# The opening of a three-block network: an input unit loaded ahead of two modulation units, and the context's affine step on ScalarE

## The chip, the cores and the metric

One core of one Trainium2 chip runs the whole program. The metric is the device time of one execution in microseconds (us). Of the kernel before, three runs are given; their median is what changes are measured against. A separate profiled execution gives the trace.

## What is computed

Three network blocks follow one another on a sequence of 256 tokens of width 1024, all in float32. The change touches the opening of the first block only:

```python
sh1, sc1, gt1, ... = split(silu(c) @ w_ada + b_ada)          # modulation of the tokens ("lat")
sh1c, sc1c, ...    = split(silu(c_ctx) @ w_ada + b_ada)      # modulation of the context ("ctx")
h_ctx = rms_norm(ctx, g_mix) * (1 + sc1c) + sh1c
h_lat = rms_norm(x, g_mix) * (1 + sc1) + sh1
u_c, q_c, v_c, ... = split_proj(h_ctx @ w_in)                # w_in: 1024 x 3072
u_l, q_l, v_l, ... = split_proj(h_lat @ w_in)
```

After it come a Fourier mixer and a gated linear recurrence over context and tokens, an output projection, a mixture of 16 experts (their weights, some 550 MB, are by far the largest part of what is read), then a second block with attention, spatial gating and a feed-forward part, and a third with two layers of attention and short convolutions.

## The kernel before, in words

**Layout.** Activations lie feature-major: 1024 features are 8 chunks of 128 partitions, 256 tokens along the free axis. `X` holds the tokens, `CTX` the context. Weights come through a ring of four slots (`ring`); a unit is what one slot holds. `w_ada`'s first 2048 columns are eight units of 1 MB (one per chunk of the input features); `w_in` is nine units of up to 384 columns (1.5 MB). The plan deals slots out in the order 2, 3, 1, 0 (`CYCLE`, line 119), so the first input unit takes the slot of modulation unit 4, the second that of unit 5, the third that of unit 6, the fourth that of unit 7. SyncE issues all these loads from one program in order; before a load it waits until the unit that had the slot has been used (`load`, L532 to L535).

**Opening.** SyncE loads X, small constants, CTX and then the modulation units (`load_ada(0)`, L558). PE sums squares of X (L893), multiplies modulation units 0 to 3 (`first_unit`, L715 to L722), sums squares of CTX, multiplies units 4 to 7, and turns the result into columns (`first_turn`, L729) after ScalarE has copied the rows out (L1391). Between them VectorE squares X (L1715), scales it by the reciprocal root (L1728, L1731), squares CTX and takes its reciprocal root too, but leaves CTX itself unscaled.

**Split weights.** A product in float32 is made of three matmuls in a reduced type: high part times high part, low times high, high times low (`parts`, L771). For every 128 columns of weights (a split, 128x1024) ScalarE copies the high part into `w_hi` (`high_parts`, L1329) and VectorE subtracts it from the weights into `ring_lo` (`low_parts`, L1706). `w_hi` has four places, so the high part of split s waits for the last block that uses split s - 4. The activations are split likewise: ScalarE copies high parts (L1408), VectorE subtracts (L1740), into `x_parts` and `ctx_parts`.

**Modulation.** `mod_in(0)` (L1770 to L1785) adds the bias to the turned columns, for the context (`modc`, L1782) and the tokens (`mod`, L1783), and two small steps (L1763) make the scales. `modulate_chunk` (L1927) is the affine step of one chunk of 128x256 on VectorE, for tokens and context. Before `mod_in(0)` VectorE makes the low parts of two splits, and that of a third after two chunks of tokens.

**Input blocks.** The first projection has 32 blocks (`in1_items`) in this order: 0 to 2 (unit 0) together, chunk by chunk (`k_outer`, L776 to L792), then 3 to 5 and 6, 7 one after another (L837), all for the tokens; then turned blocks 8 to 11, where the activation is the stationary operand (L831), for tokens and context in turn, 8 being the first turned one and 9 the first that reads the context; then 12 to 31 (L837). An unturned block is 24 matmuls, a turned one 48. Block 9 waits for all eight low chunks of the context (L912). PE also makes the bias rows after block 4 (L924), `gate_sum` after block 26 and `ada_sum` after block 29 (L754).

For each block in turn ScalarE takes the high part three splits on, evacuates the block (`evacuate`, L1335 to L1342), and in the first four blocks copies the high parts of two context chunks (L1428); at block 4 it also evacuates the bias rows (L1396). VectorE runs its own loop over the blocks (L1940 to L1956): the low part three splits on, then in the first four blocks two context chunks: two normalisations (L1945), two affine steps (L1931), two low parts (L1740). Then it adds modulation shares: the rest of `w_ada` comes as 32 tiles of 128x1024 through four buffers, each multiplied by its condition and added up on VectorE (`add_to`, L1793 to L1800) at the block that `THIRD_AT` (L126) gives it, from block 3 to block 26. SyncE loads a share (L572) when the one four before it has been added. `gate_sum` needs the last share of the gate's columns, `ada_sum` the last of all.

**Order on SyncE.** After the fourth input unit come the first four shares; later units and shares alternate by `thirds_until`, which loads a share once the block of the one four places before it is not past the block given. So all shares up to a block are waited for ahead of the next unit.

**After.** The mixers' and the output projection's PE work follows; slots of later weights come free by PE's progress, and the experts' weights stream behind them.

Of the kernel before, what the change touches and what calls it, by code (L numbers as in the profile page):

```python
# [14 lines left out]
P = 128  # L15
# [48 lines left out]
def constants():  # L64
# [21 lines left out]
    for n in range(LEVELS - 1):  # L86
# [38 lines left out]
ADA_FIRST = 2048  # L125
THIRD_AT = sorted([(3 + n, n % THIRDS, n // THIRDS) for n in range(THIRDS * KD)] +  # L126
                  [(i, THIRDS, k) for k, i in enumerate((8, 9, 10, 11, 14, 17, 20, 23))])
GATE_AT = 26
SUM_AT = 29
# [3 lines left out]
TAIL = 1  # L133
CTX_STEP = 2
CTX_ITEMS = KD // CTX_STEP
PAIRS = ATT // 2
# [120 lines left out]
def build(nc, inp, scratch, out):  # L257
# [56 lines left out]
    with ctx:  # L314
# [212 lines left out]
        def _(sp):  # L527
# [17 lines left out]
            def load_dense(units, w, after=lambda i: None):  # L545
                view = w.rearrange("(k p) n -> p k n", p=P)
                for i, g in enumerate(units):
                    load(g["u"], slot(g["u"], KD, g["w"]), view[:, :, g["c0"]:g["c0"] + g["w"]])
                    after(i)
# [7 lines left out]
            sp.dma_start(OFFS[0:33, :], inp["offsets"]).then_inc(S("rel_in"), 16)  # L557
            load_ada(0)  # L558

# [23 lines left out]

            load_dense(in1, inp["w_in"][0], after_in1)
            for kc in range(RING):
# [107 lines left out]
        def _(pe):  # L693
# [205 lines left out]
            pe.wait_ge(S("conds_ready"), 1)  # L899
            for kc in range(4):  # L900
                first_unit(kc)
            sum_squares()
            for kc in range(4, KD):
                first_unit(kc)
# [390 lines left out]
        def _(act):  # L1295
# [91 lines left out]
            root()  # L1387
            root()
            name, n = plan.used[ada[0][KD - 1]]
            act.wait_ge(S(name), n)  # L1390
# [12 lines left out]

            def high_modulated(which, c):

                src, dst = ((H, X_HI), (HC, C_HI))[which]
                act.wait_ge(S("h_chunk"), KD * which + c + 1)
                mark(act.activation(dst[:, c, :], src[:, c, :], ACT.Copy), "x_high")  # L1408

            high_parts(starts["in1"] + 3)  # L1410
            for c in range(KD):
                high_modulated(0, c)
            done = 0
            for g in in1:
                for it in g["items"]:
# [11 lines left out]
                    if done < CTX_ITEMS:  # L1427
                        for c in range(CTX_STEP):  # L1428
                            high_modulated(1, CTX_STEP * done + c)
                    if done == BROW_AT:  # L1430
# [251 lines left out]
        def _(dve):  # L1682
# [87 lines left out]
            def mod_in(p):  # L1770

                waits("turned", p + 1)
                bias = [V("b_ada", 0, 24), V("b_ada", 24, 24), V("b_ada_2", 0, 24), V("b_ada_2", 24, 24),
                        V("b_ada_3", 0, 24), mod[:, 4, :], V("b_ada_3", 24, 24)][p]
                k = 24
                if p == 0:
                    k = 16
                    bias = bias[:, 0:k]
                v = ps[:, 4, 0:4 * k].rearrange("p (q j c) -> p j q c", q=k // CG, j=CG)
                bias = bias.rearrange("p (j q) -> p j q", j=CG)  # L1780
                if p == 0:
                    link(tt(modc[:, 0:k].rearrange("p (j q) -> p j q", j=CG), v[:, :, :, 1], bias, ALU.add))  # L1782
                link(tt(mod[:, (0, 1, 2, 3, 4, 4, 5)[p], 0:k].rearrange("p (j q) -> p j q", j=CG),  # L1783
                        v[:, :, :, (0, 0, 2, 2, 3, 3, 3)[p]], bias,
                        ALU.add), "mod_ready")  # L1785

            x_squares = [0]
# [132 lines left out]
            normalise(CTX, CTX, chunks=False)  # L1920
            low_parts(starts["in1"] + 2)
            mod_in(0)
            scale_columns(V("g_mix", 0, 8), mod[:, 0, 8:16])
            scale_columns(V("g_mix", 0, 8), modc[:, 8:16])
            shift_scale = ((mod[:, 0, 0:8], scl[:, 1, :]), (modc[:, 0:8], scl[:, 2, :]))

            def modulate_chunk(which, c):  # L1927

                src, dst = ((XN, H), (CTX, HC))[which]
                shift, scale = shift_scale[which]  # L1930
                link(ts(dst[:, c, :], src[:, c, :], scale[:, c:c + 1], shift[:, c:c + 1], ALU.mult, ALU.add), "h_chunk")  # L1931

            modulate_chunk(0, 0)
            modulate_chunk(0, 1)
            low_parts(starts["in1"] + 3)
            for c in range(KD):
                if c + 2 < KD:
                    modulate_chunk(0, c + 2)
                low_modulated(c, H, X_HI, X_LO)
            for i, it in enumerate(in1_items):  # L1940
                low_parts(it["s"] + HI)
                if i < CTX_ITEMS:
                    chunks = range(CTX_STEP * i, CTX_STEP * i + CTX_STEP)
                    for c in chunks:
                        link(tt(CTX[:, c, :], CTX[:, c, :], rs[:, 0:T], ALU.mult), "normed")  # L1945
                    for c in chunks:
                        modulate_chunk(1, c)
                    for c in chunks:
                        low_modulated(c, HC, C_HI, C_LO)
                for n, (at, c, k) in enumerate(THIRD_AT):  # L1950
# [551 lines left out]
```

## Time and profile before

| | us |
|---|---|
| Median of 3 runs | 2242.11 (2239.89 to 2244.26) |
| Span of the profiled execution | 2235.1 |
| Time of the profiled execution outside its span | not given |
| PE busy | 1703.4 (76% of the span) |
| VectorE (DVE) busy | 809.1 (36%) |
| ScalarE (ACT) busy | 514.1 (23%) |
| Start of the first input block | 42.40 |
| Start of the first turned block | 74.73 |
| First expert's wait for weights in the chain | 324.56 |

The span is what the trace covers; the runs' times also hold what lies around it. Busy time is an average over very different stretches, so the trace is read by stretch. In the rows, PE is the matmul engine, PEld its weight loads, SPq what SyncE issues to the DMA queue, ACTq the same for ScalarE. L12 is line 12 of the kernel; a helper's line stands for all its uses. An arrow names what ended the idle time before an instruction. PEclk is the granted clock of TensorE: 1.00 is 2.4 GHz, 0.50 is 1.2 GHz. Instructions on one engine overlap at their ends, so the distance from start to start (the pitch) is what a step costs, rather than its duration.

### The profile page before, as it was taken

The page shows a single profiled execution, that of the slowest core. Times are in us where ns is not written, and L with a number is a line of the kernel's source. Part 1 is how long each engine was busy: PE and PEld are TensorE (multiplying, and loading weights), DVE is VectorE, ACT ScalarE, POOL GpSimd, SP SyncE. Part 2 cuts the span into 40 slices and gives each one's busy share as a digit, 9 for nine tenths or more (in the row PEclk, how much of TensorE's full clock was granted, in tenths as well). Part 3 has the DMA queues.
Part 4 walks back from the last instruction along what each step waited for, and adds up shares of the span by engine and source line. Part 5 has one row for each costly group of instructions (what it writes and reads, how often), then busy time and mean ns, then how long its engine had stood idle before and what let it go on. Part 6 is the DMA issues. An engine that isn't in the chain of part 4 may idle for free.

```text
span 2235.1 us, 33839 instructions
## 1 busy us (share of the span) xinstructions
PE 1703.4 (76%) x14882; PEld 1178.4 (53%) x14882; DVE 809.1 (36%) x1271; ACT 514.1 (23%) x833; POOL 60.7 (3%) x94
## 2 busy tenths in 40 slices
PE   5999987656656665665665666565999999999897
PEld 4896843222222321331332232222898999998897
DVE  5766730100100100010010010010875789688777
ACT  2420210000000000000000000000673664365664
POOL 0015000000000000000000000000000000000000
PEclk8999987778777777777877777787999999999998
DMA  9777989999999999999999999999645659754541
GB/s 363 294 262 298 373 354 430 434 430 433 432 431 432 431 432 435 428 432 435 430 432 433 432 432 432 431 432 402 207 148 202 198 164 368 251 169 127 167 133 66
DMA packets 138725, 760.69 MB, mean 340 GB/s; under 512 B 7911, under 2 KB 96743, under 8 KB 106888
## 3 DMA queue, kind: packets, MB, share of 16 engines
q1 hardware_dynamic: 134968, 754.13, 83.6%
q10 hardware_dynamic: 3664, 5.24, 0.7%
q8 instruction: 68, 1.11, 0.2%
q14 instruction: 25, 0.20, 0.0%
HBM read 756.20 MB, written 3.14 MB: 340 GB/s over the span
## 4 chain that ended last, share of the span: by engine, by line
DMA 48%; PE 45%; DVE 5%; ACT 1%; issue 1%; SPq 0%; DVEq 0%; ACTq 0%
DMA ring<-in_w_exp_down 26%; PE ps L837 19%; DMA ring<-in_w_exp_up 18%; PE ps L1280 4%; PE ps L1144 4%; PE ps L1137 4%; PE ps L788 3%; DMA w_hi_raw<-in_w_exp_up 3%; PE ps L710 1%; PE ps L1261 1%; PE ps L983 1%; DVE ring_lo L1706 1%; PE ps L831 1%; PE ps L1189 1%; PE ps L1200 0%
## 5 line engine op out<-in xcount | busy, mean ns | idle before, releaser
L1144 PE MATMUL ps<-arena,const 128*32 128x352 f32 x2816 | 332.1, 631 | 250.4 <-DMA arena<-in_w_exp_up 132.8
L1144 PEld LDWEIGHTS ps<-arena,const 128*32 128x32 f32 x2816 | 105.3, 140 | 466.2 <-DMA arena<-in_w_exp_up 166.1
L1706 DVE TENSOR_TENSOR ring_lo<-ring,w_hi 128x1024 fp32r<-128x1024 f32 x220 | 267.3, 1218 | 49.0 <-ACT w_hi L1329 47.9
L837 PE MATMUL ps<-u_hi,w_hi 128*128 128x258 f32 x960 | 277.2, 289 | 1.2 <-DVE ring_lo L1706 1.1
L837 PE MATMUL ps<-u_lo,w_hi 128*128 128x258 f32 x960 | 272.9, 284 | 0.0
L2111 DVE TENSOR_TENSOR tail<-tail,ps 128x704 f32<-128x704 f32 x15 | 13.3, 887 | 715.4 <-PE ps L1144 715.4
L837 PE MATMUL ps<-u_hi,ring_lo 128*128 128x258 f32 x960 | 269.2, 280 | 0.0
L1329 ACT ACTIVATE w_hi<-ring 128x1024 fp32r<-128x1024 f32 x220 | 230.1, 1050 | 72.9 <-PE ps L1280 34.6
L1144 PE MATMUL ps<-ring,const 128*32 128x352 f32 x1024 | 125.5, 654 | 80.4 <-DMA ring<-in_w_exp_up 40.2
L837 PEld LDWEIGHTS ps<-u_hi,w_hi 128*128 128x128 f32 x960 | 181.6, 189 | 7.3 <-issue 5.2
L837 PEld LDWEIGHTS ps<-u_hi,ring_lo 128*128 128x128 f32 x960 | 183.3, 191 | 0.0
L837 PEld LDWEIGHTS ps<-u_lo,w_hi 128*128 128x128 f32 x960 | 180.4, 188 | 0.0
L1137 PE MATMUL ps<-ring,const 128*32 128x256 f32 x1536 | 131.9, 513 | 57.3 <-DMA ring<-in_w_exp_down 57.2
L1137 PE MATMUL ps<-arena,const 128*32 128x256 f32 x896 | 86.5, 551 | 63.4 <-DMA arena<-in_w_exp_down 63.4
L1144 PEld LDWEIGHTS ps<-ring,const 128*32 128x32 f32 x1024 | 39.3, 144 | 167.3 <-issue 58.6
L1492 ACT ACTIVATE const<-ps 128x256 f32<-128x256 f32 x16 | 6.1, 383 | 517.3 <-PE ps L1093 517.3
L1137 PEld LDWEIGHTS ps<-ring,const 128*32 128x32 f32 x1536 | 60.5, 143 | 113.5 <-DMA ring<-in_w_exp_down 61.0
L1487 ACT ACT_TABLE_LOAD x15 | 19.2, 1283 | 405.6 <-PE ps L1144 405.6
L837 PE MATMUL ps<-x_parts,w_hi 128*128 128x256 f32 x592 | 109.2, 283 | 3.1 <-DVE ring_lo L1706 3.1
L2115 DVE TENSOR_TENSOR const<-ps,tail 128x256 f32<-128x256 f32 x15 | 6.4, 424 | 279.9 <-PE ps L1102 279.9
L1137 PEld LDWEIGHTS ps<-arena,const 128*32 128x32 f32 x896 | 42.6, 156 | 106.8 <-issue 71.4
L837 PEld LDWEIGHTS ps<-x_parts,w_hi 128*128 128x128 f32 x592 | 92.3, 188 | 6.0 <-DVE ring_lo L1706 5.5
(311 smaller groups left out, 2417.0 us busy)
## 6 DMA issues: line engine op xcount, KB each, us to landing
arena<-in_w_exp_gate SPq DMA_DIRECT2D x45, 2816.0 KB, 35.2
ring<-in_w_exp_down SPq DMA_DIRECT2D x32, 3072.0 KB, 33.0
arena<-in_w_exp_up SPq DMA_DIRECT2D x32, 2816.0 KB, 35.9
ring<-in_w_in SPq DMA_DIRECT2D x37, 1536.0 KB, 7.0
arena<-in_w_exp_down SPq DMA_DIRECT2D x16, 3072.0 KB, 36.5
ring<-in_w_exp_gate SPq DMA_DIRECT2D x15, 2816.0 KB, 30.6
ring<-in_w_exp_up SPq DMA_DIRECT2D x15, 2816.0 KB, 30.4
ring<-in_w_ada SPq DMA_DIRECT2D x24, 1536.0 KB, 7.9
```

The costliest lines, as they stand in the source:

```text
L710: m = pe.matmul(ps[32 * j:32 * j + 32, 6 + i, 0:ADA_J // 2], conds[:, kc, :], slot(u, ADA_PASS)[:, at:at + ADA_J // 2], start=(kc == first ...
L788: m = pe.matmul(ps[:, it["bank"], 0:a.shape[-1]], w, a, start=(n == 0 and j == 0), stop=(n == KD - 1 and j == 2), skip_group_check=True)
L831: m = pe.matmul(ps[:, bank, 2 * P * t:2 * P * t + 2 * P], a, w, start=(k == 0 and j == 0), stop=(k == KD - 1 and j == 2))
L837: m = pe.matmul(ps[:, bank, 0:a.shape[-1]], w, a, start=(k == 0 and j == 0), stop=(k == KD - 1 and j == 2))
L983: m = pe.matmul(o[:, :, half, :], KG[:, 4 * d + h, P * t:P * t + P], r[:, :, half, :], start=True, stop=True, skip_group_check=True)
L1137: m = pe.matmul(ps[32 * j:32 * j + 32, 4, 0:T], HIDT[:, k, :], SPACE[at][:, a:a + T], start=(k == 0), stop=(k == FC - 1), skip_group_check ...
L1144: m = pe.matmul(ps[32 * j:32 * j + 32, bank + h, 0:FJ // 2], XCUR[:, k, :], SPACE[at][:, a:a + FJ // 2], start=(k == 0), stop=(k == KD - 1 ...
L1189: m = pe.matmul(ps[:, 4 + i, T * t:T * t + T], QA[64 * i:64 * i + 64, c, P * t:P * t + P], KA[64 * i:64 * i + 64, c, :], start=True, stop= ...
L1261: m = pe.matmul(ps[:, it["b"] % 4, 0:T], w[:, it["src"], k, it["col"]:it["col"] + P], (AO, SGO)[it["src"]][:, k, :], start=(k == 0), stop= ...
L1280: m = pe.matmul(ps[:, it["b"] % 4, 0:T], w, a, start=(b == 0 and k == 0 and j == 0), stop=(b == FF // D - 1 and k == KD - 1 and j == 2), s ...
L1329: mark(act.activation(w_hi[:, s % HI, :, :], slot(c["u"], KD, c["w"])[:, :, c["col"]:c["col"] + P], ACT.Copy), "w_high")
L1706: tt(slot(c["u"], KD, c["w"], of=ring_lo)[:, :, at], slot(c["u"], KD, c["w"])[:, :, at], w_hi[:, s % HI, :, :].bitcast(F32), ALU.subtract) ...
```

## The change

- The first input unit is loaded after modulation units 0 to 5 and ahead of 6 and 7, in its old slot. PE multiplies units 0 to 5 before the context's sum of squares, and 6 and 7 after it.
- ScalarE makes the high parts of the first three splits before it copies the modulation rows out; VectorE makes their three low parts before `mod_in(0)`.
- `mod_in(0)` no longer makes the context's columns; `context_in` does, with the context's scale, after the tokens' chunks are split.
- The context is taken one chunk per block, in blocks 0 to 7 instead of two per block in 0 to 3. VectorE normalises chunk i in block i and subtracts for its low part in block i + 1; the affine step is an Identity with scale and bias on ScalarE, followed by the copy of the high part.
- The shares begin at block 5 instead of 3 and the last is added in block 28 instead of 26. The shares of the gate's columns stay.

```diff
@@ -123,16 +123,16 @@
...
 ADA_FIRST = 2048
-THIRD_AT = sorted([(3 + n, n % THIRDS, n // THIRDS) for n in range(THIRDS * KD)] +
+THIRD_AT = sorted([(5 + n, n % THIRDS, n // THIRDS) for n in range(THIRDS * KD)] +
                   [(i, THIRDS, k) for k, i in enumerate((8, 9, 10, 11, 14, 17, 20, 23))])
+FIRST_ADA = 6
 GATE_AT = 26
...
 TAIL = 1
-CTX_STEP = 2
-CTX_ITEMS = KD // CTX_STEP
+CTX_ITEMS = KD
 PAIRS = ATT // 2
@@ -555,7 +555,10 @@
...
             sp.dma_start(OFFS[0:33, :], inp["offsets"]).then_inc(S("rel_in"), 16)
-            load_ada(0)
+            load_ada(0, range(FIRST_ADA))
+            first_view = inp["w_in"][0].rearrange("(k p) n -> p k n", p=P)
+            load(in1[0]["u"], slot(in1[0]["u"], KD, in1[0]["w"]), first_view[:, :, 0:in1[0]["w"]])
+            load_ada(0, range(FIRST_ADA, KD))
 
@@ -581,7 +584,7 @@
...
 
-            load_dense(in1, inp["w_in"][0], after_in1)
+            load_dense(in1[1:], inp["w_in"][0], lambda i: after_in1(i + 1))
             for kc in range(RING):
@@ -897,10 +900,10 @@
...
             pe.wait_ge(S("conds_ready"), 1)
-            for kc in range(4):
+            for kc in range(FIRST_ADA):
                 first_unit(kc)
             sum_squares()
-            for kc in range(4, KD):
+            for kc in range(FIRST_ADA, KD):
                 first_unit(kc)
@@ -1386,6 +1389,7 @@
...
             root()
+            high_parts(starts["in1"] + 3)
             name, n = plan.used[ada[0][KD - 1]]
@@ -1401,15 +1405,20 @@
...
 
-            def high_modulated(which, c):
-
-                src, dst = ((H, X_HI), (HC, C_HI))[which]
-                act.wait_ge(S("h_chunk"), KD * which + c + 1)
-                mark(act.activation(dst[:, c, :], src[:, c, :], ACT.Copy), "x_high")
-
-            high_parts(starts["in1"] + 3)
+            def high_modulated(c):
+
+                act.wait_ge(S("h_chunk"), c + 1)
+                mark(act.activation(X_HI[:, c, :], H[:, c, :], ACT.Copy), "x_high")
+
+            def modulated_context(c):
+
+                act.wait_ge(S("normed"), KD + c + 1)
+                link(act.activation(HC[:, c, :], CTX[:, c, :], ACT.Identity, scale=scl[:, 2, c:c + 1],
+                                    bias=modc[:, c:c + 1]), "hc_chunk")
+                mark(act.activation(C_HI[:, c, :], HC[:, c, :], ACT.Copy), "x_high")
+
             for c in range(KD):
-                high_modulated(0, c)
+                high_modulated(c)
             done = 0
@@ -1425,8 +1434,7 @@
...
                     if done < CTX_ITEMS:
-                        for c in range(CTX_STEP):
-                            high_modulated(1, CTX_STEP * done + c)
+                        modulated_context(done)
                     if done == BROW_AT:
@@ -1778,11 +1786,15 @@
...
                 bias = bias.rearrange("p (j q) -> p j q", j=CG)
-                if p == 0:
-                    link(tt(modc[:, 0:k].rearrange("p (j q) -> p j q", j=CG), v[:, :, :, 1], bias, ALU.add))
                 link(tt(mod[:, (0, 1, 2, 3, 4, 4, 5)[p], 0:k].rearrange("p (j q) -> p j q", j=CG),
...
                         ALU.add), "mod_ready")
+
+            def context_in():
+
+                v = ps[:, 4, 0:64].rearrange("p (q j c) -> p j q c", q=4, j=CG)
+                link(tt(modc[:, 0:16].rearrange("p (j q) -> p j q", j=CG), v[:, :, :, 1],
+                        V("b_ada", 0, 16).rearrange("p (j q) -> p j q", j=CG), ALU.add), "modc_ready")
 
@@ -1918,35 +1930,28 @@
...
             normalise(CTX, CTX, chunks=False)
-            low_parts(starts["in1"] + 2)
+            low_parts(starts["in1"] + 3)
             mod_in(0)
             scale_columns(V("g_mix", 0, 8), mod[:, 0, 8:16])
-            scale_columns(V("g_mix", 0, 8), modc[:, 8:16])
-            shift_scale = ((mod[:, 0, 0:8], scl[:, 1, :]), (modc[:, 0:8], scl[:, 2, :]))
-
-            def modulate_chunk(which, c):
-
-                src, dst = ((XN, H), (CTX, HC))[which]
-                shift, scale = shift_scale[which]
-                link(ts(dst[:, c, :], src[:, c, :], scale[:, c:c + 1], shift[:, c:c + 1], ALU.mult, ALU.add), "h_chunk")
-
-            modulate_chunk(0, 0)
-            modulate_chunk(0, 1)
-            low_parts(starts["in1"] + 3)
+
+            def modulate_chunk(c):
+
+                link(ts(H[:, c, :], XN[:, c, :], scl[:, 1, c:c + 1], mod[:, 0, c:c + 1], ALU.mult, ALU.add), "h_chunk")
+
+            modulate_chunk(0)
+            modulate_chunk(1)
             for c in range(KD):
                 if c + 2 < KD:
-                    modulate_chunk(0, c + 2)
+                    modulate_chunk(c + 2)
                 low_modulated(c, H, X_HI, X_LO)
+            context_in()
+            scale_columns(V("g_mix", 0, 8), modc[:, 8:16])
             for i, it in enumerate(in1_items):
...
                 if i < CTX_ITEMS:
-                    chunks = range(CTX_STEP * i, CTX_STEP * i + CTX_STEP)
-                    for c in chunks:
-                        link(tt(CTX[:, c, :], CTX[:, c, :], rs[:, 0:T], ALU.mult), "normed")
-                    for c in chunks:
-                        modulate_chunk(1, c)
-                    for c in chunks:
-                        low_modulated(c, HC, C_HI, C_LO)
+                    link(tt(CTX[:, i, :], CTX[:, i, :], rs[:, 0:T], ALU.mult), "normed")
+                if 1 <= i <= CTX_ITEMS:
+                    low_modulated(i - 1, HC, C_HI, C_LO)
                 for n, (at, c, k) in enumerate(THIRD_AT):
...
```

## Rows read from the trace of the kernel before

**Rows 1.** The page: its first line.

```profile
span 2235.1 us, 33839 instructions
```

**Rows 2.** Chain of waits in order of time: start us, us, what.

```profile
27.75 7.32 DMA ring<-in_w_in
...
42.40 10.72 PE ps L788 x66
...
70.04 0.50 ACT arena L1396
...
74.73 23.06 PE ps L831 x192
...
150.83 1.43 PE ps L754 x12
...
324.56 29.73 DMA ring<-in_w_exp_down
```

**Rows 3.** Table of stretches: busy us by engine, then PEclk, DMA share, GB/s.

```profile
28.00:30.00 2.00, 2.00 (x24) 0.35 (x16) 1.53 (x1) 0.00 (x0) 0.00 (x0) 1.00 0.77 138
30.00:31.00 1.00, 0.43 (x5) 0.00 (x0) 0.00 (x0) 0.50 (x1) 0.00 (x0) 1.00 0.99 355
...
32.00:34.80 2.80, 0.21 (x2) 0.11 (x2) 0.00 (x0) 0.00 (x0) 0.00 (x0) 0.98 1.06 383
34.80:42.40 7.60, 0.00 (x1) 0.03 (x1) 5.86 (x12) 4.20 (x6) 0.00 (x0) 0.50 1.09 381
42.40:48.20 5.80, 5.80 (x27) 5.80 (x28) 5.24 (x13) 3.04 (x6) 0.00 (x0) 0.50 1.07 346
...
53.70:74.70 21.00, 16.26 (x123) 14.67 (x122) 17.43 (x30) 13.85 (x25) 0.00 (x0) 1.00 0.36 113
```

**Rows 4.** PE's waits from 54 to 158 us: us in total, times, longest.

```profile
PE ps L837 <- DVE ring_lo L1706: 3.1, 3, 1.5
PE ps L831 <- DVE ring_lo L1706: 1.7, 1, 1.7
```

**Rows 5.** Timeline of the opening: start us, us, engine, line, operation.

```profile
19.39 1.07 PE L720 MATMUL ps<-ring,conds 128*32 128x512 f32 x8 [0.93 <-DMA ring<-in_w_ada]
...
29.36 0.16 PEld L720 LDWEIGHTS ps<-ring,conds 128*32 128x32 f32 x8 [0.86 <-DMA ring<-in_w_ada]
...
31.15 1.07 PE L729 MATMUL ps<-const,rows 128*128 128x16 f32 x8 [0.72 <-ACT rows L1391]
...
38.53 0.17 DVE L1782 TENSOR_TENSOR modc<-ps,vec 128x16 f32<-128x16 f32 x1
```

**Rows 6.** Timeline of VectorE and ScalarE in one round of input blocks.

```profile
59.61 1.22 DVE L1706 TENSOR_TENSOR ring_lo<-ring,w_hi 128x1024 fp32r<-128x1024 f32 x1 [0.51 <-ACT w_hi L1329]
60.75 0.88 DVE L1945 TENSOR_TENSOR arena<-arena,rs 128x256 f32<-128x256 f32 x2
61.66 0.86 DVE L1931 TENSOR_SCALAR arena<-arena,scl,modc 128x256 f32<-128x256 f32 x2
...
62.11 0.87 ACT L1408 ACTIVATE ctx_parts<-arena 128x256 fp32r<-128x256 f32 x2 [2.34 <-DVE arena L1931]
62.88 1.04 ACT L1329 ACTIVATE w_hi<-ring 128x1024 fp32r<-128x1024 f32 x1
...
64.03 1.22 DVE L1706 TENSOR_TENSOR ring_lo<-ring,w_hi 128x1024 fp32r<-128x1024 f32 x1 [0.51 <-ACT w_hi L1329]
```

**Rows 7.** Scaled, biased Identity on ScalarE: its group by shape, and after a Sqrt.

```profile
L1351 ACT ACTIVATE arena<-tail 128x256 f32<-128x256 f32 x116 | 58.5, 509 | 104.3 <-DVE tail L1871 103.8
...
1584.04 0.40 ACT L1370 ACTIVATE rs<-rs 128x256 f32<-128x256 f32 x1
1586.15 1.31 ACT L1351 ACTIVATE arena<-tail 128x256 f32<-128x256 f32 x3 [1.71 <-DVE tail L1871]
```

**Rows 8.** VectorE's waits for modulation shares from 80 us on, and the last share.

```profile
DVE arena L1800 <- DMA arena<-in_w_ada: 23.0, 11, 5.8
...
146.43 1.28 DVE L1800 SCALAR_TENSOR_TENSOR arena<-arena,conds 128x1024 f32<-128x1024 f32 x1 [2.85 <-DMA arena<-in_w_ada]
```

## The prediction

> **What bounds the kernel now.** I began with the span and the chain of waits over all of it: the expert weights are a run of DMA pieces with short PE pieces between them, from 324.56 us on [rows 1, 2]. That stretch starts when PE starts the first expert, and PE comes to it without having waited for a transfer anywhere after the opening. So a microsecond won or lost in the opening should arrive at the end nearly whole, and a microsecond there is worth one.
>
> Then the opening. In the chain there, PE's last modulation unit hands over to a transfer of input weights (27.75, 7.32 us), and PE starts its first input block at 42.40 [rows 2]. The table of stretches shows three things [rows 3]. The DMA engines are full except for a hole at 28 to 30, because the first input unit is only issued once its slot's modulation unit has been used. PE does nothing from 32.2 to 42.4, and its granted clock falls to 0.50 (1.2 GHz) at about 34.8. It then works 5.8 us at that clock before it is back at 2.4 GHz. From 53.7 to 74.7 PE is busy 16.3 of 21.0 us. Its waits from 54 to 158 us are all for the low parts of the weights: 3.1 us in three, then 1.7 us before the first turned block at 74.73; after that there is none [rows 4].
>
> Three parts of the opening can move, then: the start at 42.40, the slow clock after it, and the 4.8 us of waits before 74.73.
>
> **Part 1, the start of block 0.** Before, the last modulation unit lands and is used at 29.36, its turn into columns ends at 31.15 + 1.07 = 32.22, but the step that reads it is only reached at 38.53, behind two low parts of weights that wait for the late transfer [rows 5]. After the change the weights are early and the modulation is late.
> - The unit of 1.57 MB goes ahead of the last two modulation units. At the 383 GB/s of 32.0 to 34.8 [rows 3] that is 4.1 us.
> - Its slot is that of modulation unit 4. Units land 2.5 us apart ((29.36 - 19.39)/4 [rows 5]), so unit 4 lands at about 21.9 and is used at about 23.0, as a unit's matmuls take 1.07 us. The hole at 28 to 30 shows some 2.2 us from such an issue (27.75) to full rate [rows 2, 3]. Unit 5, the only one still queued, ends at about 24, so the queue runs empty: 1.4 us more. (SyncE waits here with units 6 and 7 queued behind, which could have been issued before; that is what makes the hole reach them.) The last modulation unit is then ready at 29.36 + 5.5 = 34.9 (33.5 without the hole, 35.6 with all 2.2 us).
> - From there to the end of the turn was 2.86 us. But the context's sum of squares now runs behind unit 5, from 25.5 to 29.0, and then PE idles to about 32.5 for unit 6: longer than the 2.6 us after which the clock fell before. Units 6, 7 and the turn may run at 1.2 GHz; nothing to 1.3 us more, I take 0.9. Turn done at 38.6.
> - From the modulation's add to PE's first matmul were 42.40 - 38.53 = 3.87 us [rows 2, 5]. Three steps leave this stretch: the context's add and its scale (0.2 us each) and one low part (1.14 us, the pitch in [rows 6]). That leaves 2.3 us.
>
> Block 0 starts at 41.0 (38.6 to 42.0) for 42.40: **-1.4 us** (-3.8 to -0.4). The three splits are ready by then: ScalarE's three high parts from 30 to 33, VectorE's low parts to 35, both beside the transfers. ScalarE's wait for the first unit (landing at 30) sits ahead of the copy of the modulation rows, but ends some 3 us before that copy can start (23.0 + 7.3 for the transfer as before, then three high parts of 1 us: 33.3 for 36).
>
> **Part 2, the clock.** PE idles for 3.5 us before unit 6, again before unit 7 and for 2.3 us before block 0. I take the same 5.8 us at 1.2 GHz: **0** (-2.9, if it never is slow, to +0.5). The Trainium skill (TensorE: Matmul & The Clock Gate, "What's actually happening") has the slow clock as the default, released by recent activity. By that rule one can also argue that two modulation units and the turn, drawn nearer to block 0, keep the clock up; that is a rival below.
>
> **Part 3, the context's chunks.** This is the part that I expect to cost. Before, each block's round on VectorE and ScalarE went so [rows 6]: low part at 59.61, two normalisations from 60.75, two affine steps from 61.66, ScalarE's first copy at 62.11, the next high part at 62.88, the next low part at 64.03. That is a pitch of 4.42 us for two chunks, and after four blocks all eight chunks were done. After the change a block takes one chunk, but it is the same ring: VectorE does the low part and then the normalisation; ScalarE waits for that, does affine and copy, and only then the next high part, for which VectorE's next low part waits. Its pitch is 1.14 (low part) + 0.46 (one normalisation) + 0.55 (affine: the nearest row is a scaled, biased Identity of the same 128x256, 0.51 us [rows 7], plus its wait for its own end) + 0.33 (copy to high part, 62.55 to 62.88) + 1.15 (high part to low part) = **3.63 us for one chunk**. PE needs 2.88 us for a block (23.06/192 x 24 [rows 2]). So it is too slow for PE, and eight rounds long where it was four.
>
> Count from the end of block 0, t, which was 42.40 + 10.72 = 53.1. The first such low part came at 55.2 (59.61 - 4.42), t + 2.1; it becomes t + 2.4, since affine and copy take longer than the two copies did. Seven pitches on (25.4) and the bias rows' evacuation (0.50 in the chain [rows 2], taken as 0.6 with its wait), the low part of block 8's round starts at t + 28.4; with its 1.14 and the last chunk's low part 0.46 PE may start block 9, the first of the context, at t + 30.1. Before it was 74.73 + 5.8 = 80.5, or t + 27.4. The turned block 8 itself starts at about t + 22.3 for t + 21.6. Hence **+2.6 us**: PE's waits go from blocks 5 to 8 to blocks 8 (about 5 us) and 9 (2 us). Lower bound +1.8 if the affine step takes VectorE's 0.45; upper +3.7 with 0.15 more for each.
>
> The Trainium skill (ScalarE: Activation LUTs, "Rules for kernel authors") says to do multiplies and adds on VectorE, up to about 3x faster there per element in bf16. By that factor an affine step would be an estimated 1.2 us and the ring 4.3 us, some 5 us worse than my sum; the row of 0.51 us in fp32 speaks against it.
>
> **Part 4, the rest.** The modulation shares move two blocks later (first at 5, last at 28); their work on VectorE (1.3 us each at most) lies beside the handshake and beside PE. Two of the three shares that SyncE had to wait for ahead of the sixth input unit now go behind it, so it is not issued later: 0. The last share came at 146.43, the sum that needs it at 150.83 [rows 8, 2]. In block 28 it comes, after block 27's end, behind evacuation 0.28, high part 1.15, low part 1.14 and its own 1.28: 3.85 us, against two blocks' 5.75. So 1.9 us of cover is left where 3.1 was, and no cost. The context's affine leaves VectorE, where it costs nothing more; ACT has room (13.9 of 21.0 us busy [rows 3]).
>
> **Sum.** -1.4 + 0 + 2.6 = **+1.2 us** on a span of 2235.1. The profiled execution's own time is not given beside its span; the span is 7.0 us under the median of 2242.11, and I add the difference to the median: **2243.3 us**.
>
> **Rivals and chances.** About 0.2%, 4.5 us, is what a measurement of this kernel tells from no change.
> - *My forecast*, 2243.3: 0.56.
> - *The clock stays at 2.4 GHz* (no loss in units 6, 7, the turn and block 0): -2.3 - 2.9 + 2.6 = -2.6, 2239.5. For: PE is idle in shorter pieces. Against: it fell 2.6 us into a gap, and a gap of 3.5 is coming. 0.14.
> - *The first unit gains nothing at the start* (the last modulation unit is held up by the queue until block 0 starts at 42.4 again): +2.6, 2244.7. 0.07.
> - *The ring does not bind PE* (ScalarE runs ahead of VectorE, so that the 4.8 us of waits go): -1.4 - 4.8 = -6.2, 2235.9. For: the buffers are four deep and each engine alone is under PE's pace. Against: the order of the waits in the code. 0.10.
> - *Slower: the ring is longer than I price it.* Each extra microsecond in the affine step comes back seven times. From +0.5 us a round it decides (1.2 + 3.5 = 4.7); at +0.55, 2247.2. Cause could be a function table load between Silu and Identity; rows [7] show Identity soon after Sqrt without one. 0.08.
> - *Slower: the last share comes late.* VectorE waited 23.0 us in 11 waits, 5.8 at most, for shares from DMA [rows 8]. A wait of 5.8 at block 28 is 3.9 us over the cover: 1.2 + 3.9, 2247.2. It decides from 5.3 us. 0.05.
>
> Range: start bounds and the clock rival give 2238.0 at the low end; the two slower rivals and my upper bounds 2247.5. Faster is the fourth alone, 0.10; slower the last two, 0.13; within 0.2% the rest, 0.77.
>
> **What would show it.** Right: block 0 at 40 to 42; the granted clock at 0.50 around it; low parts in blocks 1 to 8 at a pitch of 3.6 us with VectorE waiting for w_hi; a PE wait of about 5 us for ring_lo before the first turned matmul and one of 2 us for the context's low parts before the second; the sum of shares on time. Wrong: a clock of 1.00 at block 0 (part 2), low parts under 3 us apart (part 3), or a last modulation unit before 33 or after 36 us (part 1). More than 5 us either way would mean that a step outside these moved, above all the transfers.

## The result, and the profile after the change

The changed kernel took 2247.41 us in the median of 20 runs (2239.42 to 2251.6), the kernel before 2242.86 on the same chip. The ratio is 1.0021, with an interval of 1.0013 to 1.003: **slower by some 4.7 us** (2.9 to 6.7), where +1.2 was forecast, inside what counted as no change. The prediction gave 0.13 to a kernel slower by more than 0.2%.

The span of the profiled execution is 2247.8 us, its own time 2249.57. In the runs of this study the time lies 1.8 to 2.2 us over the span, so the profiled execution of before (span 2235.1) took about 2237, near the low end of its runs, and not the median. Runs of one kernel lie some 10 us apart here. The two profiled executions part mostly after the opening: from PE's last input blocks to the first expert's wait for weights it is 172.3 us before (152.26 to 324.56) and 180.6 after (156.16 to 336.76). One stretch shows the granted clock in it, in the table of stretches (busy us by engine, then PEclk, DMA share, GB/s), first after, then before:

```profile
200.00:220.00 20.00, 19.07 (x142) 14.20 (x135) 9.41 (x14) 1.41 (x2) 4.54 (x9) 0.76 0.80 316
```

```profile
200.00:220.00 20.00, 19.07 (x184) 14.31 (x187) 10.62 (x17) 2.54 (x4) 1.03 (x4) 1.00 0.94 363
```

PE is busy alike, the clock is 0.76 for 1.00. One kernel can show both: in e9 and e12 below, which are the same code, it is 0.69 and 1.00 in this stretch, and the way to the first expert takes 179.4 and 174.9 us. So the two spans, 12.7 us apart, say little; the opening is compared by the places of its pieces in the chain, and the time by medians.

The chain of waits after, in order of time (start, us, what), answers to [rows 2]:

```profile
22.27 1.11 PE ps L723 x8
23.40 0.38 SPq L535
23.82 0.58 SPq L535
24.44 10.95 DMA ring<-in_w_ada
35.44 1.98 PE ps L723 x8
37.44 0.61 ACT rows L1395
38.09 1.90 PE ps L732 x8
...
42.34 10.40 PE ps L791 x66
...
75.95 25.73 PE ps L834 x192
101.69 42.71 PE ps L840 x360
...
154.73 1.43 PE ps L757 x12
156.16 5.91 PE ps L840 x48
```

The first input unit is early, but block 0 starts at 42.34, where it started at 42.40. The turned blocks start at 75.95 for 74.73, and the last input blocks' piece at 156.16; before it was at 152.26 (150.83 and 1.43 [rows 2]). The opening lost 3.9 us, and the medians do not show that the rest gave it back. Which stretch lost what can be seen in the stretches of [rows 3], now:

```profile
24.00:25.00 1.00, 0.27 (x4) 0.16 (x8) 0.93 (x3) 0.00 (x0) 0.00 (x0) 1.00 0.83 49
...
34.80:42.40 7.60, 3.88 (x17) 2.07 (x17) 3.19 (x8) 1.85 (x4) 0.00 (x0) 0.50 1.10 381
42.40:48.20 5.80, 5.80 (x30) 5.80 (x31) 5.27 (x15) 3.04 (x6) 0.00 (x0) 0.56 1.05 352
...
53.70:74.70 21.00, 16.00 (x120) 14.29 (x119) 10.71 (x17) 14.70 (x25) 0.00 (x0) 1.00 0.24 77
74.70:80.50 5.80, 4.55 (x21) 4.55 (x22) 4.52 (x7) 2.81 (x6) 0.00 (x0) 0.51 0.99 305
```

The hole in the transfers is still there, only sooner: 49 GB/s from 24 to 25. The clock stands at 0.50 (1.2 GHz) from 34.8 to block 0, which now holds the last modulation unit and its turn. And there is something new: VectorE's work from 53.7 to 74.7 fell from 17.4 to 10.7 us, yet PE did no more, and after 74.7 the clock is at 0.51. Before the change it was at 1.00 there:

```profile
74.70:80.50 5.80, 5.77 (x48) 5.77 (x49) 5.80 (x6) 0.57 (x1) 0.00 (x0) 1.00 0.97 311
```

PE's waits from 30 to 170 us (us in total, times, longest) and one round of the changed ring (start, us, engine, line; then the idle time before) answer to [rows 4, 6]:

```profile
PE ps L834 <- DVE ring_lo L1714: 5.3, 1, 5.3
PE ps L723 <- DMA ring<-in_w_ada: 4.9, 2, 3.5
PE ps L791 <- DVE x_parts L1748: 2.4, 1, 2.4
PE ps L840 <- DVE ring_lo L1714: 0.8, 2, 0.6
```

```profile
60.44 0.60 ACT L1416 ACTIVATE arena<-arena,modc,scl 128x256 f32<-128x256 f32 x1 [1.43 <-DVE arena L1952]
61.07 0.42 ACT L1418 ACTIVATE ctx_parts<-arena 128x256 fp32r<-128x256 f32 x1
61.39 1.04 ACT L1332 ACTIVATE w_hi<-ring 128x1024 fp32r<-128x1024 f32 x1
...
72.80 0.42 ACT L1418 ACTIVATE ctx_parts<-arena 128x256 fp32r<-128x256 f32 x1
72.81 0.67 ACTq L1405 DMA_DIRECT2D bias_rows<-arena  x1
73.58 1.06 ACT L1332 ACTIVATE w_hi<-ring 128x1024 fp32r<-128x1024 f32 x1 [0.36 <-issue]
```

The ring is there as forecast: affine, copy, high part on ScalarE, then VectorE's low part and normalisation, then affine again. From copy to high part it takes 0.32 us (61.07 to 61.39), but 0.78 where ScalarE also issues the transfer of bias rows (72.80 to 73.58): that instruction was in no term of the prediction.

### The profile page after: what moved, and what is told of

Same layout as the page of the kernel before. It is cut to its first block, busy times and chain, and to the rows that moved or that the text cites. A ratio compares the mean times of both kernels' runs of the same rounds, so it can differ in the third digit from the quotient of the medians.

```text
span 2247.8 us, 33841 instructions
## 1 busy us (share of the span) xinstructions
PE 1711.5 (76%) x14882; PEld 1186.9 (53%) x14882; DVE 805.9 (36%) x1263; ACT 519.5 (23%) x841; POOL 60.8 (3%) x94
## 4 chain that ended last, share of the span: by engine, by line
DMA 49%; PE 44%; DVE 4%; ACT 1%; issue 1%; SPq 1%; DVEq 0%; ACTq 0%
DMA ring<-in_w_exp_down 27%; PE ps L840 19%; DMA ring<-in_w_exp_up 16%; DMA w_hi_raw<-in_w_exp_up 5%; PE ps L1283 4%; PE ps L1147 4%; PE ps L791 3%; PE ps L1140 3%; PE ps L713 2%; PE ps L986 1%; PE ps L1264 1%; PE ps L834 1%; DVE ring_lo L1714 1%; DMA ring<-in_w_ada 1%; PE ps L1192 1%
## 5 line engine op out<-in xcount | busy, mean ns | idle before, releaser
L1140 PE MATMUL ps<-ring,const 128*32 128x256 f32 x1536 | 126.0, 495 | 61.8 <-DMA ring<-in_w_exp_down 61.8
```

What stands on the lines that cost most here:

```text
L1140: m = pe.matmul(ps[32 * j:32 * j + 32, 4, 0:T], HIDT[:, k, :], SPACE[at][:, a:a + T], start=(k == 0), stop=(k == FC - 1), skip_group_check ...
```

## The experiments

All were timed against the kernel before on the same chip. "Last piece" is the start of PE's last input blocks in the chain (152.26 before, 156.16 after). "From block 0" is the time from block 0's end to it, which leaves the start and block 0's own clock out. The fourth column is the ratio's interval times 2242.9.

| kernel | median us | ratio, 95% interval | time to before, us | last piece to before, us | from block 0, us |
|---|---|---|---|---|---|
| before | 2242.25 to 2243.71 | 1 | 0 | 0 | 99.1 |
| after | 2247.41 | 1.0021 (1.0013 to 1.003) | +2.9 to +6.7 | +3.9 | 103.4 |
| e1_loads_only | 2244.05 | 1.0002 (0.9992 to 1.0013) | -1.8 to +2.9 | -0.3 | 99.2 |
| e2_context_only | 2244.71 | 1.0017 (1.0004 to 1.003) | +0.9 to +6.7 | +4.3 | 103.4 |
| e3_affine_vector | 2245.19 | 1.0011 (0.9999 to 1.0022) | -0.2 to +4.9 | +2.4 | 101.9 |
| e4_two_chunks | 2240.61 | 0.9993 (0.9984 to 1.0001) | -3.6 to +0.2 | +3.0 | 102.6 |
| e5_norms_first | 2236.32 | 0.9976 (0.9962 to 0.999) | -8.5 to -2.2 | -6.1 | 94.8 |
| e6_after_unit6 | 2246.38 | 1.0018 (1.0007 to 1.0029) | +1.6 to +6.5 | +6.6 | 103.7 |
| e7_both | 2236.08 | 0.9972 (0.9959 to 0.9984) | -9.2 to -3.6 | -4.9 | 95.3 |
| e8_shares_back | 2246.73 | 1.0014 (1.0003 to 1.0025) | +0.7 to +5.6 | +4.8 | 104.0 |
| e9_old_loads | 2235.87 | 0.9985 (0.9972 to 0.9997) | -6.3 to -0.7 | -4.1 | 94.5 |
| e10_before_norms | 2238.74 | 0.9987 (0.9969 to 1.0004) | -7.0 to +0.9 | -2.3 | 96.5 |
| e11_pair_early | 2235.7 | 0.9966 (0.9953 to 0.9979) | -10.5 to -4.7 | -4.1 | 94.5 |
| e12_pair_late | 2236.39 | 0.9969 (0.9957 to 0.9981) | -9.6 to -4.3 | -3.5 | 96.0 |

The last two columns are one execution each. Of the same code, e5 and e11 stand 2.1 us apart in the last piece, but all of that lies before block 0's end: from there on they take 94.8 and 94.5 us, and before and e1, or after and e2, agree within 0.1. With that, the last piece's move lies inside the time's interval in nine rows of thirteen; in e6, e11 and e12 it lies 0.1 to 0.8 us outside, in e4 2.8. In e9 the medians lie 6.4 us apart (2242.25 for the kernel before beside it), just outside what the ratio's interval gives.

### Which half costs: e1 and e2

e1 is the kernel before with the new order of loads, of PE's units, of the high parts and of the low parts ahead of the modulation; e2 is the changed kernel with these undone.

```diff
+            load_ada(0, range(FIRST_ADA))
+            load(in1[0]["u"], slot(in1[0]["u"], KD, in1[0]["w"]), first_view[:, :, 0:in1[0]["w"]])
+            load_ada(0, range(FIRST_ADA, KD))
...
+            high_parts(starts["in1"] + 3)
```

> The new order of loads alone; context as before the change (two chunks per block, affine on VectorE, shares from block 3). Theory R (the round between VectorE and ScalarE, eight times instead of four, is the cost): block 0 at about 42.7 us, block 12 at 97.5 to 98.5 for 97.79 before, ratio 0.999 to 1.001. Rival S (late modulation units and PE at 1.2 GHz through them are the cost): block 12 at 101 or later, ratio 1.002.

> The context's part and the later shares alone, with the loads in the order of before. R: block 0 at about 42.0, low parts in blocks 1 to 8 at a pitch of 3.7 us and more, block 12 at 101 to 102, ratio 1.002. S: block 12 at about 98, ratio 1.000.

With before and after, these make a square: last piece at 152.26 (before), 151.99 (loads alone), 156.54 (context alone), 156.16 (both). The context's part costs 4.2 to 4.3 us, whichever the loads are, and it is the same 4.3 from block 0's end on (99.1 and 99.2 for 103.4 and 103.4). The loads' 0.3 to 0.4 us lies before block 0's end and is less than two executions of one kernel differ by there. In e1 block 0 starts at 42.10, and PE's waits are those of before, 3.1 and 1.7 us. In e2 they are those of after:

```profile
PE ps L831 <- DVE ring_lo L1711: 5.3, 1, 5.3
PE ps L837 <- DVE ring_lo L1711: 0.8, 2, 0.6
```

### The engine of the affine step, and the number of chunks: e3 and e4

e3 has the affine step on VectorE again, behind the normalisation, still one chunk a block; e4 leaves it on ScalarE and takes two chunks in each of four blocks.

```diff
+                    link(ts(HC[:, i, :], CTX[:, i, :], scl[:, 2, i:i + 1], modc[:, i:i + 1], ALU.mult, ALU.add), "h_chunk")
```

```diff
-CTX_ITEMS = KD
+CTX_STEP = 2
+CTX_ITEMS = KD // CTX_STEP
```

> The changed kernel with the context's affine step back on VectorE, still one chunk per block. R: the round only shortens by the difference of the two steps (0.64 on ScalarE to 0.46 on VectorE), pitch 3.5 for 3.7, block 12 at about 100.3 for 101.7, ratio 1.001 to 1.002. Rival A (the affine step's engine is the cost): back to 98, ratio 1.000.

> The changed kernel with two chunks per block on ScalarE, so four rounds. R: a round of 4.7 us, four of them, block 8 at about 76.5, block 9 follows it without a wait (context ready early), block 12 at about 99.8, ratio 1.001. Rival A: no better than the changed kernel, 1.002 or more.

One round of e3, on VectorE:

```profile
58.02 1.22 DVE L1712 TENSOR_TENSOR ring_lo<-ring,w_hi 128x1024 fp32r<-128x1024 f32 x1 [1.04 <-ACT w_hi L1332]
59.16 0.42 DVE L1950 TENSOR_TENSOR arena<-arena,rs 128x256 f32<-128x256 f32 x1
59.62 0.41 DVE L1951 TENSOR_SCALAR arena<-arena,scl,modc 128x256 f32<-128x256 f32 x1
60.06 0.43 DVE L1746 TENSOR_TENSOR ctx_parts<-arena,ctx_parts 128x256 fp32r<-128x256 f32 x1
61.53 1.23 DVE L1712 TENSOR_TENSOR ring_lo<-ring,w_hi 128x1024 fp32r<-128x1024 f32 x1 [1.04 <-ACT w_hi L1332]
```

Its pitch is 3.51 us for the changed kernel's 3.70: the affine step takes 0.44 from start to start on VectorE and 0.63 on ScalarE, so the engine is worth 0.2 us a round, 1.5 us in all (last piece at 154.63). The eight rounds remain. In e4 a round of two chunks takes 4.64 us, for 4.42 before, and the last piece comes at 155.26; 1.5 us of its delay is block 8, which took 7.3 us for 5.8 with the clock at 0.50 from 78 to 80. Its median, though, is the lowest of the kernels with the changed ring (after, e2, e3, e6, e8 and it), and its opening doesn't explain that. Its twelve runs lie within 2.9 us (2239.3 to 2242.24), where after, e2, e3, e6 and e8 spread over 8 to 13, and its profiled execution, at 2241.9, has its first expert's wait at 329.14, 4.6 us later than before the change. So that execution does show the loss; why the slower runs of the others are missing here stays open.

### Taking the ring apart: e5 and e10

VectorE idles in block 0, from 49.7 to 55.1 in the changed kernel. e5 puts all eight normalisations there; then no step of VectorE stands between its low part and ScalarE's affine step. e10 makes the same edit in the kernel before, and nothing else.

```diff
-                if i < CTX_ITEMS:
-                    link(tt(CTX[:, i, :], CTX[:, i, :], rs[:, 0:T], ALU.mult), "normed")
+                for c in range(KD if i == 0 else 0):
+                    link(tt(CTX[:, c, :], CTX[:, c, :], rs[:, 0:T], ALU.mult), "normed")
```

> The changed kernel, but VectorE normalises all eight context chunks in block 0, where it stood idle for over 5 us, instead of one per block. ScalarE's affine step then waits for nobody. R (the round is the cost): no wait of PE for low parts from block 3 to 9, block 12 starts about 49.5 us after block 0 (59.4 in the changed kernel, 55.4 before the change), at about 92; ratio 0.997 to 0.998. Rival A (ScalarE's extra work is the cost): block 12 stays at 100 or later, ratio 1.002.

> The kernel before, with one edit: VectorE does all eight normalisations of the context in block 0, where it idles, instead of two in each of blocks 0 to 3. Affine steps stay on VectorE, two chunks a block, loads as before. Theory (the round of low part, context work, copy, high part bounds the first blocks, whichever engine does the affine step): the pitch of the low parts falls by two normalisations, from 4.42 to about 3.5 us, in blocks 1 to 3, so about 2.7 of PE's 4.8 us of waits go, and the time is 2240.2 (2238.1 if all 4.8 go). Rival A: the affine step on ScalarE is needed too for the gain of e5_norms_first; the waits stay at 4 to 5 us and the time at 2242.9. Rival B: the longer work in block 0 delays the first low parts, and nothing is gained or 1 to 2 us lost.

VectorE in e5:

```profile
48.94 3.64 DVE L1952 TENSOR_TENSOR arena<-arena,rs 128x256 f32<-128x256 f32 x8
53.75 1.23 DVE L1714 TENSOR_TENSOR ring_lo<-ring,w_hi 128x1024 fp32r<-128x1024 f32 x1 [1.17 <-ACT w_hi L1332]
54.90 0.42 DVE L1748 TENSOR_TENSOR ctx_parts<-arena,ctx_parts 128x256 fp32r<-128x256 f32 x1
55.91 1.23 DVE L1714 TENSOR_TENSOR ring_lo<-ring,w_hi 128x1024 fp32r<-128x1024 f32 x1 [0.60 <-ACT w_hi L1332]
```

The pitch is 2.16 us, which is ScalarE's own work without a wait, and under PE's 2.88. PE's waits for low parts from block 3 on are down to 0.4 us, the last piece starts at 146.14, 10.0 us before the changed kernel's, and the time is 2236.32: the same instructions, eight of them moved, make it faster than both kernels. That the ring is what cost is thereby shown: ScalarE's extra work, the rival, is all still in e5. In e10 the pitch in blocks 1 to 3 fell from 4.42 to 3.50, as expected, and the last piece came 2.3 us earlier; the median is 3.5 us lower, but the interval reaches to +0.9.

### The first unit one place later, the shares back: e6, e7, e8

e6 loads the first input unit behind modulation unit 6 (`FIRST_ADA = 7`), to let SyncE issue that unit before it waits for the slot. e7 is e5 with this edit; e8 gives the shares their old blocks.

```diff
-FIRST_ADA = 6
+FIRST_ADA = 7
```

```diff
-THIRD_AT = sorted([(5 + n, n % THIRDS, n // THIRDS) for n in range(THIRDS * KD)] +
+THIRD_AT = sorted([(3 + n, n % THIRDS, n // THIRDS) for n in range(THIRDS * KD)] +
```

> The changed kernel with the first input unit behind modulation unit 6, ahead of unit 7 alone. H (the hole in the transfers, from waiting for the slot of unit 4 with nothing queued, holds the modulation back): the last modulation unit is ready at about 34 for 35.4, block 0 at 40.5 to 41.5 for 42.3, block 12 at 100 to 101. Rival (the queue was full): block 0 unchanged. Ratio 1.001 to 1.002 either way.

> Both edits: all normalisations in block 0 and the first unit behind unit 6. R and H: block 0 at 40.5 to 41.5, block 12 at 90 to 91.5, ratio 0.996 to 0.998. If only R holds, block 12 at 92; if neither, 100.

> The changed kernel with the modulation shares from block 3 on again. R: VectorE has over 1 us idle in each round, so shares there cost nothing: block 12 at 101 to 102, ratio 1.001 to 1.003. Rival D (the later shares hold back VectorE or SyncE later in the projection): the stretch from block 12 to the end of the projection (60.4 us) gets shorter, ratio 1.000.

e6 missed. The hole did not go, it moved, and in this execution unit 7 was only ready at 37.55 and block 0 started at 44.45. But e7 has the same order of loads, and there they were at 35.59 and 42.12. So e6 shows no gain from the later place, and its late start is not shown to come from it. The stretches of e6:

```profile
26.00:27.00 1.00, 1.00 (x8) 0.00 (x0) 0.00 (x0) 0.00 (x0) 0.00 (x0) 0.50 1.03 93
27.00:28.00 1.00, 0.54 (x4) 0.00 (x0) 0.00 (x0) 0.00 (x0) 0.00 (x0) 0.50 0.74 227
```

e7 is not told apart from e5, and e8 (last piece 157.01) not from the changed kernel: the shares' two blocks are worth nothing that shows, as Part 4 had it. In e8 VectorE has a share's 0.76 us in the round from 62.85 to 66.48, and that round takes 3.63 us, no more than one without a share.

### Is the early unit worth anything once the ring is gone: e9, e11, e12

e9 is e5 with the order of loads of before. Its profile stood 2.1 us behind e5's while the medians agreed, so both were run again on one chip, as e11 (early unit) and e12 (old order).

> The changed kernel with all eight normalisations of the context in block 0 (as in e5_norms_first), but with the loads, PE's order and the low parts ahead of the modulation as they were before the change. Theory: the early first unit is worth nothing, also when the ring no longer binds PE. Block 0 at 42.1 to 43.0, the last blocks' piece of PE in the chain at 146 to 147 us, time within 1.5 us of e5_norms_first's 2236.3. Rival A: the early unit is worth its 1.4 us or more once nothing behind it takes it back: the last piece 1.4 to 3 us later than in e5_norms_first (147.5 to 149), time 2237.7 to 2239.5. Rival B: the early unit costs (its hole in the transfers): 1 to 2 us below e5_norms_first.

> e5_norms_first again, now on the same chip as e12_pair_late, to see what the early first unit is worth where the ring doesn't bind PE. The two profiles so far put the last blocks' piece of PE 2.1 us apart (146.14 for 148.20), but the medians, from different chips, stand at 2236.3 and 2235.9. Theory (worth nothing that lasts): the two medians agree within 1 us. Rival (worth 2 us): this one is 1.5 to 3 us faster than e12_pair_late, and its last piece again starts some 2 us earlier, 146 for 148.

> e9_old_loads again, beside e11_pair_early. Theory: the same median within 1 us. Rival: 1.5 to 3 us slower, the last blocks' piece of PE at about 148 us, block 0 at 43 us and 10.5 us long where it was 42.0 and 9.4 with the early unit.

2235.70 and 2236.39: within 1 us, and the last pieces lie 0.6 us apart (148.21 and 148.78). With nine and six runs a gain of 2 us or so could still hide in this. All the profiles together say the same: block 0 ended at 51.36 to 53.75, median 52.74, in the seven executions with the first unit behind modulation unit 5, and at 52.77 to 53.75, median 53.13, in the five with the old order. No gain of the early first unit can be told from nothing, with the ring or without it. Block 0 started at 44.33 in e11, 2.3 us later than the same code did in e5: the last modulation unit was taken up 1.3 us later (37.42 for 36.08), and it ran at half the clock (1.94 us for 1.06). That unit, which the change put behind the input unit, is what the start hangs on. In e12, and by 0.8 and 0.2 us in e7 and e5, a limit shows that the last rival foresaw for another case, a share late at the sum:

```profile
PE ps L754 <- DVE arena L1809: 1.5, 1, 1.5
```

## Why the prediction was wrong, point by point

The direction of the sum was right and the ring was found; two terms were mis-sized, both the same way, by 1.6 and 1.3 us, of which 0.3 came back in a third. What failed is the price of the ring, because a step that lies in it was left out, and next to it the price of the slow clock ahead of block 0.

**Part 3, the context's chunks: +2.6 was forecast, +4.2 came, and this term decided.** Block 9, the first of the context, was to start 30.1 us after block 0's end; it starts at 84.35, that is 31.6 after 52.74. Before it was 80.53, or 27.4 after 53.12. Low parts stand at 55.14 (2.4 after block 0's end, as forecast), 58.84, 62.54, 66.25, 70.58, 74.67, 78.66 and 82.64: 27.5 us in seven pitches, for 26.0 in the working. Two steps make up the difference, and a third that might have did not.
- The affine step: 0.63 from start to start (60.44 to 61.07) for 0.55; the first pitches are 3.70 for 3.63, in all 0.5 us. The row of 509 ns in [rows 7] was near, but that Identity has other operands; this one takes 0.60 by itself.
- The bias rows' transfers, issued by ScalarE in three rounds: pitches of 4.09, 3.99 and 3.98 for 3.70, together 1.0 us. **This is the failed step.** The prediction priced the bias rows' evacuation (0.63 us in the round of 4.33, taken as 0.6) and not the three issues that follow it in blocks 5 to 7. Before, they stood behind the last chunk of the context (from 70.57 on), where ScalarE had no ring to hold up; with eight rounds they stand inside it. No run takes these transfers out; what speaks for them is the rows. The shares that VectorE adds in the same three rounds are not the cause, since the round of e8 that has a share and no transfer takes 3.63 us; and in e5, where ScalarE alone sets the pitch, the three rounds with a transfer take 2.64, 2.51 and 2.53 us from high part to high part for 2.16.
- The function table load for Silu (1.28 us at 66.16) cost nothing: VectorE's low part and normalisation ran beside it, and the affine step would not have started before 67.84 in any case.

The waits were placed otherwise than forecast, though. Block 8 waited 5.3 us (about 5 was forecast); block 9 did not wait its 2 us. In the wait the granted clock fell, and block 8 ran at 1.2 GHz for most of its 8.4 us (75.95 to 84.35), for 5.8 before. That filled the time until the last chunk of the context was ready (its low part is made from 83.79 to 84.21). So the slow clock is hidden behind the ring in the changed kernel, and a kernel that only shortens the ring does not get all of it back: in e3 the last chunk was ready at 82.25, and block 9 started at 82.91. In e4 the context was ready at 71.9, and block 9 came at 83.54, behind block 8's 7.3 us.

**Part 1, the start: -1.4 was forecast, -0.1 came.** Much of the working held. The last modulation unit was to be ready at 34.9, and PE took it up at 35.44. From the modulation's add to the first matmul it is 2.32 us (40.02 to 42.34), for 2.3 forecast. What failed is the 0.9 us for the slow clock: these rows show unit 6, unit 7 and the turn.

```profile
32.95 1.06 PE L723 MATMUL ps<-ring,conds 128*32 128x512 f32 x8 [3.50 <-DMA ring<-in_w_ada]
35.44 1.93 PE L723 MATMUL ps<-ring,conds 128*32 128x512 f32 x8 [1.43 <-DMA ring<-in_w_ada]
37.44 0.60 ACT L1395 ACTIVATE rows<-ps 128x512 f32<-128x512 f32 x1 [4.05 <-PE ps L723]
38.09 1.89 PE L732 MATMUL ps<-const,rows 128*128 128x16 f32 x8 [0.72 <-ACT rows L1395]
```

Unit 6 still had the full clock, but unit 7 and the turn each cost 0.8 to 0.9 us more than their 1.07: 1.7 us for 0.9. With the 0.5 by which unit 7 was late, that is the missing 1.3. This is one execution of a start that moved by 2.3 us between two of the same code; that the start gained next to nothing is borne out by the ends of block 0 above.

**Part 2, the clock: 0 was forecast, -0.3 came.** Block 0 takes 10.40 us for 10.72. The rival in which the clock stays at 2.4 GHz did not come about here. In e5 it nearly did: the granted clock is 1.00 from 34 to 38 and 0.76 from 42 to 48, and block 0 takes 9.36. In e11, the same code, the start was late. PE's wait just ahead of block 0 was 2.4 us in all three, so its length alone doesn't tell the clock behind it.

**Part 4, the rest: 0 was forecast and came**, by e8. The late share was no rival in the changed kernel, where PE did not wait for it.

**The sum.** -0.1 - 0.3 + 4.2 = +3.8 at block 9, and +3.9 at the last piece. The medians' +4.7 (2.9 to 6.7) agrees. **The reference point:** the difference was added to the median of before, as it should be. Of the 7.0 us between span and median, which it left open, only some 1.8 lie around the span; the rest is how that execution differed from the median.

**The rivals.** The one that came nearest is "the ring is longer than I price it", which had 0.08 and was to decide from +0.5 us a round. The rounds measured +0.2 on average over the priced ones (1.5 us in seven), and the cause it named as possible, a function table load, cost nothing; the rest came from Part 1, whose rival "the first unit gains nothing" had 0.07. Each alone would have been no change; together they were not listed. The Trainium skill (ScalarE: Activation LUTs, "Rules for kernel authors") puts adds and multiplies on VectorE, where in bf16 they are up to about 3 times faster per element. In fp32 here the direction holds (0.44 us on VectorE in e3, 0.63 on ScalarE), with a factor of 1.4.

## What to carry to other kernels

Moving a step to a freer engine need do nothing for a ring that alternates between two engines, and here it made each round 0.2 us longer. Count the hand-overs in a round and the number of rounds, and ask which step can be done before the ring starts (eight normalisations moved into an idle stretch brought the last input blocks from 3.9 us behind the kernel before to 6.1 ahead of it). When a ring is stretched over more blocks, look at everything that the engine's program does in the added blocks, transfers that it issues included. A load drawn ahead pushes another back: find out which of the two the start hangs on.

## What was not expected of the hardware

- A transfer issued by ScalarE went with 0.25 to 0.36 us of idle time ahead of its next instruction ([0.36 <-issue] above), and with 0.3 to 0.4 us more in its round.
- A wait of PE of 4.9 to 5.3 us (after, e2, e3, e6, e8) was followed by a granted clock of 0.50 in the block behind it; a wait of 1.7 us (before, e1, e10) by 1.00. In e4, after a wait of 2.0 us with 4.6 us of shorter ones ahead of it, it fell too, 0.6 us into the block; before and e1 had 3.1 us of shorter ones. The slow clock cost the block 1.5 to 2.7 us (7.3 to 8.5 us for 5.8) on top of the wait.
- e11 and e5, the same code, started block 0 at 44.33 and at 42.00. One profile does not tell a change of 2 us in this opening; the time from block 0's end on, 94.8 and 94.5 us, told more.
